# The third sum of weight blocks moves from VectorE to GpSimd in a two-block transformer kernel, and the opening splits its first gate block before it sums

## The chip, the cores and the metric

The kernel runs on one core of a Trainium2 chip. The metric is device time in microseconds (us) of one execution, the median of three runs. TensorE is written PE, VectorE DVE, ScalarE ACT, GpSimd POOL and SyncE SP.

## The reference

Two blocks follow each other, each of two layers, on 256 tokens of width 1024, all in float32. The first block's layer has a feed-forward part (FFN), a mixer of neighbourhood attention and a Fourier transform, and a second FFN; the second block's layer has a mixer of four parts and one FFN. So there are six FFNs:

```python
def swiglu(x, w_in, w_out):
    gu = x @ w_in
    g, u = jnp.split(gu, 2, axis=-1)
    return (jax.nn.silu(g) * u) @ w_out

for l in range(DEPTH):
    x = x + 0.5 * swiglu(rms_norm(x, ffn1_norm[l]), ffn1_w_in[l], ffn1_w_out[l])
    x = x + mixer(rms_norm(x, mix_norm[l]), ...)
    x = x + 0.5 * swiglu(rms_norm(x, ffn2_norm[l]), ffn2_w_in[l], ffn2_w_out[l])
...
    x = x + (jax.nn.silu(gate) * up) @ w_down[l]
```

with `w_in` of 1024 x 5632 and `w_out` of 2816 x 1024.

## The kernel before

**Three products for one.** A float32 weight block `w` is split into `whi` (rounded to the fast matmul type fp32r, by ACT) and `wlo` = `w` - `whi` (by DVE); the activations are split in the same way (`xTh`, `xTl`, `bTh`, `bTl`). Each product is three matmuls: hi by hi, hi by lo and lo by hi (lines L2263 to L2265).

**Units.** The weights of an FFN stream through three slots of 128 x 2048 as 42 "units". For unit u: SP loads it into `raw` (L602) or into a buffer in `work` (L628), ACT rounds it (`hi`, L1100), DVE takes the rest (`lo`, L1616), PE uses it in 12 or 24 matmuls of 128 x 512. The slot of unit u is free when PE has finished unit u - 3. The semaphores `w_hi_ready`, `w_lo_ready` and `unit_done` count units.

**Fewer products by sums of blocks.** Most of `w_in` is multiplied in three groups (i = 0, 1, 2) in the manner of Strassen: of the four blocks of a group (gate and up, upper and lower half of the rows: gate_k0, gate_k1, up_k0, up_k1) seven products are made, five with a sum of blocks or a block alone that is not straight from `raw`:

```python
SUM_UNITS = ((4, 6, 8, 9, 11, 13, 15), (16, 18, 20, 21, 23, 25, 27), (28, 30, 32, 33, 35, 37, 38))
```

For group i these are units m = 0 to 6: m = 0 is gate_k0; m = 1 is the first sum `w_sum` = gate_k0 + up_k0 (L1631); m = 2 is gate_k1; m = 3 is the second sum `t2` = `w_sum` + up_k1 (L1638); m = 4 is the third sum up_k0 + up_k1 (L1641), which is written into `w_sum` again; m = 5 is up_k1; m = 6 is `t2` with gate_k1 added to it by a DMA that POOL issues (`added_block`, L830). All three sums are 128 x 2048 additions on DVE. PE's results are combined by short DVE instructions that read one operand from PSUM (`combine_z` L1656, `combine_u` L1660, `combine_w` L1664, `combine_up0` L1672, `combine_gate1` L1676). `form` and `form_lo_part` (L1710, L1714) make the matching sums of activations, once for each FFN; `product` (L1687) and `pair_product` (L1681) are the gated products.

**Order.** Every engine's program is written out by hand and runs in order. On DVE, within group i, the third sum stands behind `combine_z(i)` and, in group 0, behind two more splits. PE's unit m = 4 of a group starts with a wait for `combine_w(i)`. SP loads up_k0 of the next group when the third sum of this one is done, and up_k1 of the next group when the lo part of m = 5 is done. In the first FFN (f = 0, `start`), the first group's gate and up blocks are loaded after the opening's chunks. POOL's program holds small norm instructions, DMA issues for the attention tables (`spread_table`, seven of them, each waiting for one unit of PE; `attention_bias`, 16 pairs, likewise, in the first FFN of each layer of the first block), four mask additions and `added_block`.

Of the kernel before, what the change touches and what calls it, by code (L numbers as in the profile page):

```python
# [23 lines left out]
ALU = mybir.AluOpType  # L24
# [53 lines left out]
Z_AT, U_AT, W_AT, UP1_AT, UP0_AT, GATE1_AT = 1, 2, 3, 4, 5, 6  # L78
SUMS = 3
T1_AT, T2_AT, T3_AT = 1, 2, 3  # L80
FORMS = 4
# [95 lines left out]
class Signals:  # L177


    def __init__(self, sem):  # L180
# [18 lines left out]
        self.gain_f_landed = sem("gain_f_landed")  # L199
        self.gate_bias_landed = sem("gate_bias_landed")  # L200
        self.small_landed = sem("small_landed")
# [148 lines left out]
def build(nc, a, out):  # L350

    with ExitStack() as ctx:
# [66 lines left out]
        zw, up1 = xn[:, 0, 0:BANK], xn[:, 0, BANK:D]  # L419
        up_k0, up_k1, w_sum, t2 = (area(at, UNIT) for at in (4096, 6144, 8192, 10240))  # L420
        x_full = xn[:, :, :].rearrange("p t d -> p (t d)").rearrange("p (k t n) -> p k t n", k=KC, t=TT)
# [140 lines left out]
        def _(sp):  # L562
# [31 lines left out]
            def ffn(w_in, w_out, l, rnd, f, beside={}):  # L594
# [65 lines left out]
                for i in range(GROUPS):  # L660
                    if i:
                        sp.wait_ge(s.w_sum_ready, SUMS * (GROUPS * f + i - 1) + T3_AT)
                    if rnd == 0 and i == 0:
                        sp.wait_ge(raw_landed[0], 64)
                    up_block(i, 0, up_k0)
                    gate_block(i, 0)
                    if i:
                        sp.wait_ge(s.w_lo_ready, unit(0, rnd) + SUM_UNITS[i - 1][5] + 4)
                        up_block(i, 1, up_k1)
                    plain(2 + i, 0)  # L670
                    if i == 0:
                        up_block(i, 1, up_k1)
                    plain(2 + i, 1)
                    gate_block(i, 1)
                    for d in range(3 * i, 3 * i + 3):
                        if d != 2 + 3 * i or i < GROUPS - 1:
                            down(d)
# [3 lines left out]
            for l in range(DEPTH):  # L681
# [19 lines left out]
                def gate_bias(t, half):  # L701
                    at = half * D
                    broadcast(gate[:, t, at:at + D], "mix_gate_bias", l * 2 * D + at, D, s.gate_bias_landed)

# [86 lines left out]
        def _(pool):  # L791
# [20 lines left out]

            def spread_table(l, rnd):

                with nc.allow_non_contiguous_dma(reason="rows of 64 keys"):
                    for dr in range(NA_DR):
                        pool.wait_ge(s.unit_done, unit(1, rnd) + dr + 4)
                        src = bass.AP(tensor=a["na_rpb"].tensor,
                                      offset=l * (NA_H * RPB_R * RPB_C) + (dr + 8 - GRID_H) * RPB_C + RPB_C // 2,
                                      ap=[[RPB_R * RPB_C, NA_H], [-1, GRID_W], [1, GRID_W]])  # L820
                        dst = spread[:, l * NA_H:(l + 1) * NA_H, dr * GRID_W:(dr + 1) * GRID_W]
                        pool.dma_start(dst.rearrange("q h k -> h q k"), src).then_inc(s.rpb_spread, LOADED)

            def added_block(name, l, rnd, i):
# [8 lines left out]
            def attention_bias(l, rnd):  # L833
# [3 lines left out]
                for j in range(BANDS):  # L837
                    for row in range(GRID_H):
                        if (j, row) == (2, 1):
                            added_block("ffn1_w_in", l, rnd - 4, 1)  # L840
# [8 lines left out]
            for l in range(DEPTH):  # L849
                (r1, _, _, _), (r2, _, _, _) = ffn_stages_a(l)  # L850
                norm(3 * l)
                if l == 0:
                    spread_table(0, r1)
                added_block("ffn1_w_in", l, r1, 0)
                attention_bias(l, r1 + 4)
                pool.wait_ge(s.consts_a_landed, 16)
                pool.wait_ge(s.bias_landed, 2 * BANDS * GRID_H * LOADED * (l + 1))
# [32 lines left out]
                if l + 1 < DEPTH:  # L890
                    spread_table(l + 1, r2)
                for i in range(GROUPS):
                    added_block("ffn2_w_in", l, r2, i)
            pool.wait_ge(s.gain_m_landed, 16 * (DEPTH + 1))
# [7 lines left out]
            for l in range(DEPTH):  # L902
# [102 lines left out]
        def _(act_e):  # L1005
# [85 lines left out]
            def ffn(rnd, f, n, o):  # L1091
# [15 lines left out]
                def summed_hi(i, m):  # L1107
                    source, at = {1: (w_sum, T1_AT), 3: (t2, T2_AT), 4: (w_sum, T3_AT), 6: (t2, 0)}[m]
                    if at:
# [402 lines left out]
        def _(v):  # L1512
# [94 lines left out]
            def ffn(rnd, f, n, o, factor, start=False, next_gain=None):  # L1607
# [13 lines left out]
                def summed_lo(i, m):  # L1621
                    lo(SUM_UNITS[i][m], {1: w_sum, 3: t2, 4: w_sum, 5: up_k1, 6: t2}[m])

# [9 lines left out]
                def second_sum(i):  # L1633
# [4 lines left out]
                    v.tensor_tensor(t2, w_sum, up_k1, ALU.add).then_inc(s.w_sum_ready, 1)  # L1638

                def third_sum(i):  # L1640
                    v.tensor_tensor(w_sum, up_k0, up_k1, ALU.add).then_inc(s.w_sum_ready, 1)  # L1641

# [89 lines left out]
                form_lo_part(1)  # L1732
                first_sum(0)
                for i in range(GROUPS):
                    qa, qb = PLAIN_UNITS[2 + i]
                    loaded_lo(SUM_UNITS[i][0])
                    if i == 0:
                        product_lo(0)
                    loaded_lo(qa)
                    if i == 0:  # L1740
# [16 lines left out]
                    combine_z(i)  # L1757
                    if i == 0:
                        summed_lo(i, 3)
                        loaded_lo(DOWN_UNITS[3 * i])  # L1760
                        third_sum(i)
                        product(2 + i, 0)
                    else:
                        third_sum(i)
                        product(2 + i, 0)
                        summed_lo(i, 3)
                        loaded_lo(DOWN_UNITS[3 * i])
                    if i:
                        product_lo(3 * i)
                    product(2 + i, 1)  # L1770
                    combine_u(i)
                    summed_lo(i, 4)
                    if i:
                        product_lo(3 * i + 1)
                    combine_w(i)
                    loaded_lo(DOWN_UNITS[3 * i + 1])
                    summed_lo(i, 5)
# [57 lines left out]
            def mixer_a(l, next_gain):  # L1835
# [31 lines left out]
                v.wait_ge(s.bias_masked, BANDS * (l + 1))  # L1867
                v.wait_ge(s.gate_bias_landed, 64 * l + 64)

# [1039 lines left out]
```

## Time and profile before

| | |
|---|---|
| median of 3 runs | 1581.43 us (1580.72 to 1581.44) |
| the profiled execution | 1581.31 us, its span 1579.5 us |
| PE busy | 1563.9 us, 99% |
| DVE busy | 1274.1 us, 81% |
| ACT busy | 902.0 us, 57% |
| POOL busy | 219.9 us, 14% |
| mean granted PE clock | 0.999 |
| third sums on DVE | 18, mean 2.28 us |

The span is what the profiler saw; the execution's own time is 1.8 us longer. An engine's rows are stamped with start and duration. The ends of matmuls are modelled: a 128 x 512 matmul is shown as 0.39 us, while the next one starts 0.23 us after it. So a pause of PE is 0.16 us longer, start to start, than the idle time shown. DVE's instructions are shown to start up to 0.1 us before the one ahead of them ends.

### The profile page before, as it was taken

How to read it: one execution, taken by the hardware profiler on the slowest of the kernel's cores; microseconds unless marked ns; L12 is line 12 of the kernel's file. 1: busy time of each engine (PE TensorE's matmuls, PEld its weight loads, DVE VectorE, ACT ScalarE, POOL GpSimd, SP SyncE). 2: the span in 40 equal slices, each digit the busy share in tenths (PEclk: the TensorE clock that was granted, in tenths of full speed). 3: DMA queues.
4: the chain of work that ended last, by engine and by line, in shares of the span. 5: the costliest groups of instructions: out<-in, count | busy, mean ns of one | idle time of the engine just before them, and what ended most of it. 6: DMA issues, size and time to landing. Idle time of an engine off the chain costs nothing.

```text
span 1579.5 us, 18791 instructions
## 1 busy us (share of the span) xinstructions
PE 1563.9 (99%) x7346; PEld 1294.5 (82%) x7346; DVE 1274.1 (81%) x1181; ACT 902.0 (57%) x1000; POOL 219.9 (14%) x271
## 2 busy tenths in 40 slices
PE   8999999999999999999999999999999999999998
PEld 6888888888888888888888888888888888888886
DVE  7888856679887989875677988778898876798886
ACT  7555555646555655555565655566655556665554
POOL 1132112011000113211201000131200002110000
PEclk9999999999999999999999999999999999999999
DMA  9987665558766778766456776561877565277662
GB/s 302 279 230 219 230 210 164 185 183 248 246 196 177 241 233 248 215 223 212 156 178 211 255 237 211 161 220 54 266 231 230 191 192 172 96 260 231 192 210 91
DMA packets 182415, 327.29 MB, mean 207 GB/s; under 512 B 13028, under 2 KB 77944, under 8 KB 182328
## 3 DMA queue, kind: packets, MB, share of 16 engines
q1 hardware_dynamic: 169064, 300.66, 57.2%
q0 software_dynamic: 12960, 24.94, 8.7%
q8 instruction: 58, 0.95, 0.3%
q10 hardware_dynamic: 304, 0.50, 0.1%
q14 instruction: 29, 0.24, 0.0%
HBM read 322.88 MB, written 2.88 MB: 206 GB/s over the span
## 4 chain that ended last, share of the span: by engine, by line
PE 92%; DVE 3%; ACT 2%; issue 1%; DMA 1%; SPq 0%; POOLq 0%; POOL 0%; ACTq 0%; DVEq 0%
PE pg L2263 19%; PE pg L2265 19%; PE pg L2264 19%; PE acc L2263 9%; PE acc L2265 9%; PE acc L2264 9%; PE pg L2384 2%; ACT whi L1100 1%; PE pg L2276 1%; DVE wlo L1616 1%; DVE work L1641 1%; DMA raw<-in_ffn_w_in 1%; PE acc L2557 0%; PE acc L2539 0%; PE acc L2728 0%
## 5 line engine op out<-in xcount | busy, mean ns | idle before, releaser
L2263 PE MATMUL pg<-whi,xTh 128*128 128x512 f32 (+1 forms) x1096 | 436.2, 398 | 4.2 <-DVE wlo L1616 2.5
L2265 PE MATMUL pg<-whi,xTl 128*128 128x512 f32 (+1 forms) x1096 | 426.5, 389 | 0.0
L2264 PE MATMUL pg<-wlo,xTh 128*128 128x512 f32 (+1 forms) x1096 | 425.7, 388 | 0.0
L1616 DVE TENSOR_TENSOR wlo<-raw,whi 128x2048 fp32r<-128x2048 f32 x143 | 328.8, 2299 | 52.4 <-ACT whi L1100 48.7
L1100 ACT ACTIVATE whi<-raw 128x2048 fp32r<-128x2048 f32 x143 | 274.1, 1917 | 153.7 <-PE pg L2265 99.4
L1516 DVE TENSOR_TENSOR wlo<-raw,whi 128x2048 fp32r<-128x2048 f32 (+1 forms) x87 | 198.5, 2282 | 59.4 <-ACT whi L1012 59.2
L2263 PEld LDWEIGHTS pg<-whi,xTh 128*128 128x128 f32 x1096 | 205.9, 188 | 48.9 <-DVE wlo L1616 3.0
L2265 PEld LDWEIGHTS pg<-whi,xTl 128*128 128x128 f32 x1096 | 205.7, 188 | 42.5
L2264 PEld LDWEIGHTS pg<-wlo,xTh 128*128 128x128 f32 x1096 | 206.1, 188 | 40.0 <-issue 1.0
L1616 DVE TENSOR_TENSOR wlo<-work,whi 128x2048 fp32r<-128x2048 f32 x90 | 208.2, 2313 | 31.4 <-ACT whi L1100 31.4
L2263 PE MATMUL acc<-whi,bTh 128*128 128x512 f32 (+1 forms) x572 | 227.2, 397 | 0.0
L1100 ACT ACTIVATE whi<-work 128x2048 fp32r<-128x2048 f32 x90 | 172.5, 1917 | 90.9 <-PE acc L2265 50.9
L2265 PE MATMUL acc<-whi,bTl 128*128 128x512 f32 (+1 forms) x572 | 222.8, 389 | 0.0
L2264 PE MATMUL acc<-wlo,bTh 128*128 128x512 f32 (+1 forms) x572 | 222.3, 389 | 0.0
L1012 ACT ACTIVATE whi<-raw 128x2048 fp32r<-128x2048 f32 (+1 forms) x87 | 165.0, 1899 | 61.8 <-PE acc L2265 37.0
L2265 PEld LDWEIGHTS acc<-whi,bTl 128*128 128x128 f32 x572 | 107.3, 188 | 22.9
L2263 PEld LDWEIGHTS acc<-whi,bTh 128*128 128x128 f32 x572 | 107.5, 188 | 21.4 <-DVE bTl L1694 0.7
L2264 PEld LDWEIGHTS acc<-wlo,bTh 128*128 128x128 f32 x572 | 107.6, 188 | 20.6
L1156 ACT ACTIVATE bTh<-pg 128x512 fp32r<-128x512 f32 x66 | 39.3, 596 | 75.6 <-PE pg L2384 75.6
L2263 PE MATMUL pg<-whi,bTh 128*128 128x512 f32 (+1 forms) x178 | 70.1, 394 | 3.0 <-DVE xn L1664 3.0
L2265 PE MATMUL pg<-whi,bTl 128*128 128x512 f32 (+1 forms) x178 | 69.2, 389 | 0.0
L2264 PE MATMUL pg<-wlo,bTh 128*128 128x512 f32 (+1 forms) x178 | 69.1, 388 | 0.0
(276 smaller groups left out, 1962.0 us busy)
## 6 DMA issues: line engine op xcount, KB each, us to landing
raw<-in_ffn_w_in SPq DMA_DIRECT2D x124, 512.0 KB, 5.6
raw<-in_ffn_w_out SPq DMA_DIRECT2D x88, 512.0 KB, 4.5
raw<-in_mix_w_in SPq DMA_DIRECT2D x64, 512.0 KB, 4.7
raw<-in_w_gate_up SPq DMA_DIRECT2D x64, 512.0 KB, 5.4
work<-in_ffn_w_in SPq DMA_DIRECT2D x48, 512.0 KB, 5.8
raw<-in_w_down SPq DMA_DIRECT2D x44, 512.0 KB, 4.4
work<-in_ffn_w_in POOLq DMA_DIRECT2D x24, 512.0 KB, 8.5
raw<-in_w_in SPq DMA_DIRECT2D x24, 512.0 KB, 5.4
```

Of the source, the lines that this page charges most:

```text
L1012: act_e.activation(whi[:, slot, 0:cols], raw[:, slot, 0:cols], ACT.Copy).then_inc(s.w_hi_ready, 1)
L1100: act_e.activation(whi[:, u % SLOTS, :], source, ACT.Copy).then_inc(s.w_hi_ready, 1)
L1156: act_e.activation(bTh[:, part, :], bank[:, :].rearrange("p (c n) -> p c n", c=2), ACT.Copy).then_inc(s.actT_hi, 1)
L1516: v.tensor_tensor(wlo[:, slot, 0:cols], raw[:, slot, 0:cols], f32(whi[:, slot, 0:cols]), ALU.subtract)\
L1616: v.tensor_tensor(wlo[:, u % SLOTS, :], source, f32(whi[:, u % SLOTS, :]), ALU.subtract).then_inc(s.w_lo_ready, 1)
L1641: v.tensor_tensor(w_sum, up_k0, up_k1, ALU.add).then_inc(s.w_sum_ready, 1)
L2263: pe.matmul(dst, xh, wh, start=first and i == 0, stop=False, skip_group_check=onto)
L2264: pe.matmul(dst, xh, wl, start=False, stop=False, skip_group_check=onto)
L2265: mm = pe.matmul(dst, xl, wh, start=False, stop=last and i == len(pairs) - 1, skip_group_check=onto)
L2276: tr = pe.transpose(pg[b][t][:, c * P:(c + 1) * P], xn[:, t, at:at + P], ident[:, :])
L2384: tr = pe.transpose(bank[:, c * T + t * P:c * T + (t + 1) * P], source[:, t, at + c * P:at + (c + 1) * P], ident[:, :])
```

## The change

The third sum gets a buffer of its own, `t3`, at the free place 2048 of `work`, a semaphore of its own, `third_ready`, and is made by POOL. It is released when both up blocks have landed (and for i > 0 when the previous third sum's lo part is done), rather than by its place in DVE's order. `w_sum` and its counter keep two sums. SP waits for the second sum and the third before it reloads up_k0. In group 0 the two `product`s of the group's plain block move behind `combine_w(0)`. In the first FFN, SP loads the gate block before the up block, DVE makes the lo part of unit 4 before the first sum that also reads that block, and SP waits for the first sum before it overwrites the slot. `gate_bias_landed` is merged into `chunk_landed[3]` to free the semaphore.

```diff
-SUMS = 3
-T1_AT, T2_AT, T3_AT = 1, 2, 3
+SUMS = 2
+T1_AT, T2_AT = 1, 2
...
-        up_k0, up_k1, w_sum, t2 = (area(at, UNIT) for at in (4096, 6144, 8192, 10240))
+        t3, up_k0, up_k1, w_sum, t2 = (area(at, UNIT) for at in (2048, 4096, 6144, 8192, 10240))
...
                     if i:
-                        sp.wait_ge(s.w_sum_ready, SUMS * (GROUPS * f + i - 1) + T3_AT)
+                        sp.wait_ge(s.w_sum_ready, SUMS * (GROUPS * f + i - 1) + T2_AT)
+                        sp.wait_ge(s.third_ready, GROUPS * f + i)
                     if rnd == 0 and i == 0:
                         sp.wait_ge(raw_landed[0], 64)
-                    up_block(i, 0, up_k0)
-                    gate_block(i, 0)
+                        gate_block(i, 0)
+                        up_block(i, 0, up_k0)
+                    else:
+                        up_block(i, 0, up_k0)
+                        gate_block(i, 0)
...
+                    if rnd == 0 and i == 0:
+                        sp.wait_ge(s.w_sum_ready, T1_AT)
                     gate_block(i, 1)
...
                     for dr in range(NA_DR):
+                        if dr == 4:
+                            third_sum(f, rnd, 0)
                         pool.wait_ge(s.unit_done, unit(1, rnd) + dr + 4)
...
+            def third_sum(f, rnd, i):
+
+                for half in range(2):
+                    pool.wait_ge(chunk_landed[half], 16 + 32 * (GROUPS * f + i + 1))
+                if i:
+                    pool.wait_ge(s.w_lo_ready, unit(0, rnd) + SUM_UNITS[i - 1][4] + 4)
+                pool.tensor_tensor(t3, up_k0, up_k1, ALU.add).then_inc(s.third_ready, 1)
...
                     for row in range(GRID_H):
+                        if (j, row) == (1, 2):
+                            third_sum(2 * l, rnd - 4, 1)
                         if (j, row) == (2, 1):
...
                 if l == 0:
-                    spread_table(0, r1)
+                    spread_table(0, r1, 0)
+                else:
+                    third_sum(2 * l, r1, 0)
                 added_block("ffn1_w_in", l, r1, 0)
                 attention_bias(l, r1 + 4)
+                third_sum(2 * l, r1, 2)
...
                 for i in range(GROUPS):
+                    if i or l + 1 == DEPTH:
+                        third_sum(2 * l + 1, r2, i)
                     added_block("ffn2_w_in", l, r2, i)
...
                 for i in range(GROUPS):
+                    third_sum(2 * DEPTH + l, ffn_stage_b(l)[0], i)
                     added_block("w_gate_up_2", l, ffn_stage_b(l)[0], i)
...
-
-                def third_sum(i):
-                    v.tensor_tensor(w_sum, up_k0, up_k1, ALU.add).then_inc(s.w_sum_ready, 1)
...
-                first_sum(0)
+                if start:
+                    loaded_lo(SUM_UNITS[0][0])
+                    first_sum(0)
+                else:
+                    first_sum(0)
+                    loaded_lo(SUM_UNITS[0][0])
...
                     combine_w(i)
+                    if i == 0:
+                        product(2, 0)
+                        product(2, 1)
```

DVE's program at the opening of the first FFN, before. `xn`, `bTh`, `raw`, `work` and `whi` are buffers in SBUF, `pg` is PSUM; L1714 is `form_lo_part`, L1631 the first sum, L1616 a lo split (units 4 and 5 here), L1694 `product_lo`, L1687 `product(1, ...)`, L1638 the second sum:

```order
L1714 TENSOR_TENSOR bTl<-xn,bTh 128x512 x2
L1631 TENSOR_TENSOR work<-raw,work 128x2048
L1616 TENSOR_TENSOR wlo<-raw,whi 128x2048
L1694 TENSOR_TENSOR bTl<-pg,bTh 128x512
L1616 TENSOR_TENSOR wlo<-raw,whi 128x2048
L1687 SCALAR_TENSOR_TENSOR work<-pg,rstd,work 128x256 x2
L1638 TENSOR_TENSOR work<-work 128x2048
```

And of the change (L1737, L1642, L1657, L1717, L1710 and L1664 of the changed kernel are the same instructions):

```order
L1737 TENSOR_TENSOR bTl<-xn,bTh 128x512 x2
L1642 TENSOR_TENSOR wlo<-raw,whi 128x2048
L1657 TENSOR_TENSOR work<-raw,work 128x2048
L1717 TENSOR_TENSOR bTl<-pg,bTh 128x512
L1642 TENSOR_TENSOR wlo<-raw,whi 128x2048
L1710 SCALAR_TENSOR_TENSOR work<-pg,rstd,work 128x256 x2
L1664 TENSOR_TENSOR work<-work 128x2048
```

The split of unit 4 and the first sum have changed places; what follows is as it was.

DVE's program from `combine_z(0)` (L1656) to `combine_w(0)` (L1664) of any FFN, before; L1641 is the third sum, the two L1687 the products of the plain block:

```order
L1656 TENSOR_TENSOR xn<-pg,p 128x512
L1616 TENSOR_TENSOR wlo<-work,whi 128x2048
L1616 TENSOR_TENSOR wlo<-raw,whi 128x2048
L1641 TENSOR_TENSOR work<-work 128x2048
L1687 SCALAR_TENSOR_TENSOR xn<-pg,rstd,xn 128x256 x2
L1660 TENSOR_TENSOR p<-pg,p 128x512
L1616 TENSOR_TENSOR wlo<-work,whi 128x2048
L1664 TENSOR_TENSOR xn<-xn,pg 128x512
L1616 TENSOR_TENSOR wlo<-raw,whi 128x2048
```

And of the change:

```order
L1679 TENSOR_TENSOR xn<-pg,p 128x512
L1642 TENSOR_TENSOR wlo<-work,whi 128x2048
L1642 TENSOR_TENSOR wlo<-raw,whi 128x2048
L1683 TENSOR_TENSOR p<-pg,p 128x512
L1642 TENSOR_TENSOR wlo<-work,whi 128x2048
L1687 TENSOR_TENSOR xn<-xn,pg 128x512
L1710 SCALAR_TENSOR_TENSOR xn<-pg,rstd,xn 128x256 x2
L1642 TENSOR_TENSOR wlo<-raw,whi 128x2048
```

The sum is gone and the two products stand behind `combine_w`.

POOL's program in the first FFN, before; L822 are the issues of `spread_table`, L830 `added_block`, L847 `attention_bias`, L864 the mask additions:

```order
L805 TENSOR_TENSOR rstd<-ms,neghalf 128x1
L822 DMA rpb_spread<-in_na_rpb 8x64x64 x7
L830 DMA work<-in_ffn_w_in 128x2x512 x2
L847 DMA shared<-rpb_spread 16x4x256 x18
L830 DMA work<-in_ffn_w_in 128x2x512 x2
L847 DMA shared<-rpb_spread 16x4x256 x14
L864 TENSOR_TENSOR shared<-shared,consts_a 128x16x32
```

And of the change, where L838 is the third sum:

```order
L811 TENSOR_TENSOR rstd<-ms,neghalf 128x1
L830 DMA rpb_spread<-in_na_rpb 8x64x64 x4
L838 TENSOR_TENSOR work<-work 128x2048
L830 DMA rpb_spread<-in_na_rpb 8x64x64 x3
L846 DMA work<-in_ffn_w_in 128x2x512 x2
L865 DMA shared<-rpb_spread 16x4x256 x12
L838 TENSOR_TENSOR work<-work 128x2048
L865 DMA shared<-rpb_spread 16x4x256 x6
L846 DMA work<-in_ffn_w_in 128x2x512 x2
L865 DMA shared<-rpb_spread 16x4x256 x14
L838 TENSOR_TENSOR work<-work 128x2048
L885 TENSOR_TENSOR shared<-shared,consts_a 128x16x32
```

The three sums stand behind the issue that waits for unit 4, behind the pair that waits for unit 17, and behind the pair that waits for unit 27.

## Rows read from the trace of the kernel before

**Rows 1.** The page: busy time of each engine, share, instructions

```profile
PE 1563.9 (99%) x7346; PEld 1294.5 (82%) x7346; DVE 1274.1 (81%) x1181; ACT 902.0 (57%) x1000; POOL 219.9 (14%) x271
```

**Rows 2.** Waits of PE: us in total, times, longest us

```profile
PE pg L2263 <- DVE xn L1664: 3.0, 6, 0.5
PE pg L2263 <- DVE wlo L1616: 2.5, 1, 2.5
```

**Rows 3.** Timeline, opening: ACT on unit 4, `product(1)`, PE's units 5 and 6

```profile
29.34 1.90 ACT L1100 ACTIVATE whi<-raw 128x2048 fp32r<-128x2048 f32 x1
...
29.89 2.29 DVE L1631 TENSOR_TENSOR work<-raw,work 128x2048 f32<-128x2048 f32 x1
...
37.09 0.87 DVE L1687 SCALAR_TENSOR_TENSOR work<-pg,rstd,work 128x256 f32<-128x256 f32 x2
...
38.02 0.50 PE L2263 MATMUL pg<-whi,xTh 128*128 128x512 f32 x1 [0.57 <-DVE work L1687]
...
44.06 0.39 PE L2263 MATMUL pg<-whi,bTh 128*128 128x512 f32 x1
```

**Rows 4.** Groups of POOL's additions by size: xcount | busy us, mean ns

```profile
L885 POOL TENSOR_TENSOR work<-work 128x126 f32<-128x126 f32 x8 | 3.6, 452 | 0.0
...
L877 POOL TENSOR_TENSOR work<-work 128x512 f32<-128x512 f32 x2 | 2.6, 1296 | 0.2
```

**Rows 5.** Timeline, POOL's first two mask additions beside DVE

```profile
147.60 2.29 DVE L1616 TENSOR_TENSOR wlo<-work,whi 128x2048 fp32r<-128x2048 f32 x1 [0.26 <-ACT whi L1100]
...
148.15 2.88 POOL L864 TENSOR_TENSOR shared<-shared,consts_a 128x512 f32<-128x512 f32 x1 [15.19 <-PE pg L2265]
150.02 3.16 DVE L1616 TENSOR_TENSOR wlo<-raw,whi 128x2048 fp32r<-128x2048 f32 x1
...
154.03 1.29 POOL L864 TENSOR_TENSOR shared<-shared,consts_a 128x512 f32<-128x512 f32 x1 [0.56 <-PE pg L2265]
...
154.10 0.67 DVE L1660 TENSOR_TENSOR p<-pg,p 128x512 f32<-128x512 f32 x1
```

**Rows 6.** Line L628, load of up_k1(0), third FFN: issue times, landing

```profile
L628 SPq DMA_DIRECT2D work<-in_ffn_w_in x2: 469/488/508, 532.3 to 532.9; - x2
...
DMA to landing us min/median/max: 6.0/6.4/6.8
```

**Rows 7.** Timeline, third FFN: lo part of unit 5, and PE on it

```profile
545.29 2.28 DVE L1616 TENSOR_TENSOR wlo<-raw,whi 128x2048 fp32r<-128x2048 f32 x1
...
548.52 0.40 PE L2263 MATMUL pg<-whi,xTh 128*128 128x512 f32 x1
```

**Rows 8.** Timeline, second FFN: fourth issue of `spread_table`, lo of unit 6, PE

```profile
369.35 0.80 POOL L822 DMA_DIRECT2D rpb_spread<-in_na_rpb  x1 [2.48 <-PE pg L2265]
370.32 2.28 DVE L1616 TENSOR_TENSOR wlo<-work,whi 128x2048 fp32r<-128x2048 f32 x1
...
374.31 0.39 PE L2263 MATMUL pg<-whi,bTh 128*128 128x512 f32 x1
```

**Rows 9.** Timeline, first FFN, group 2: POOL behind unit 27, `combine_gate1`, PE's unit 30

```profile
131.95 1.02 POOL L847 DMA_DIRECT2D shared<-rpb_spread  x2 [1.71 <-PE pg L2265]
...
133.19 0.68 DVE L1676 TENSOR_TENSOR p<-pg,p 128x512 f32<-128x512 f32 x1
...
139.65 0.39 PE L2263 MATMUL pg<-whi,bTh 128*128 128x512 f32 x1
```

**Rows 10.** Timeline, first FFN, group 1: POOL behind unit 17, `pair_product`, PE's unit 20

```profile
92.27 1.01 POOL L847 DMA_DIRECT2D shared<-rpb_spread  x2 [4.42 <-PE pg L2265]
...
93.21 0.74 DVE L1681 SCALAR_TENSOR_TENSOR work<-xn,rstd,work 128x512 f32<-128x512 f32 x1
...
99.97 0.39 PE L2263 MATMUL pg<-whi,xTh 128*128 128x512 f32 x1
```

**Rows 11.** Timeline, second FFN, group 1: first sum, and PE's unit 15

```profile
402.03 2.28 DVE L1631 TENSOR_TENSOR work<-raw,work 128x2048 f32<-128x2048 f32 x1
...
411.20 0.39 PE L2263 MATMUL pg<-whi,xTh 128*128 128x512 f32 x1
```

More of the change, by code:

```diff
@@ L199, in __init__ @@
         self.gain_f_landed = sem("gain_f_landed")
-        self.gate_bias_landed = sem("gate_bias_landed")
+        self.third_ready = sem("third_ready")
         self.small_landed = sem("small_landed")
@@ L702, in gate_bias @@
                     at = half * D
-                    broadcast(gate[:, t, at:at + D], "mix_gate_bias", l * 2 * D + at, D, s.gate_bias_landed)
+                    broadcast(gate[:, t, at:at + D], "mix_gate_bias", l * 2 * D + at, D, chunk_landed[3])
                 ffn("ffn1_w_in", "ffn1_w_out", l, r1, 2 * l,
@@ L811, in norm, with spread_table @@
                           2 * n + t + 1)
-            def spread_table(l, rnd):
+            def spread_table(l, rnd, f):
                 with nc.allow_non_contiguous_dma(reason="rows of 64 keys"):
                     for dr in range(NA_DR):
+                        if dr == 4:
+                            third_sum(f, rnd, 0)
                         pool.wait_ge(s.unit_done, unit(1, rnd) + dr + 4)
@@ L890, in _ @@
                 if l + 1 < DEPTH:
-                    spread_table(l + 1, r2)
+                    spread_table(l + 1, r2, 2 * l + 1)
                 for i in range(GROUPS):
+                    if i or l + 1 == DEPTH:
+                        third_sum(2 * l + 1, r2, i)
                     added_block("ffn2_w_in", l, r2, i)
@@ L1107, in summed_hi @@
                 def summed_hi(i, m):
-                    source, at = {1: (w_sum, T1_AT), 3: (t2, T2_AT), 4: (w_sum, T3_AT), 6: (t2, 0)}[m]
-                    if at:
+                    source, at = {1: (w_sum, T1_AT), 3: (t2, T2_AT), 4: (t3, 0), 6: (t2, 0)}[m]
+                    if m == 4:
+                        act_e.wait_ge(s.third_ready, GROUPS * f + i + 1)
+                    elif at:
                         act_e.wait_ge(s.w_sum_ready, SUMS * (GROUPS * f + i) + at)
@@ L1621, in summed_lo @@
                 def summed_lo(i, m):
-                    lo(SUM_UNITS[i][m], {1: w_sum, 3: t2, 4: w_sum, 5: up_k1, 6: t2}[m])
+                    lo(SUM_UNITS[i][m], {1: w_sum, 3: t2, 4: t3, 5: up_k1, 6: t2}[m])
                 def sums_before(i):
@@ L1732, in ffn @@
                 form_lo_part(1)
-                first_sum(0)
+                if start:
[4 more added lines that the diff above has]
+                    loaded_lo(SUM_UNITS[0][0])
                 for i in range(GROUPS):
                     qa, qb = PLAIN_UNITS[2 + i]
-                    loaded_lo(SUM_UNITS[i][0])
                     if i == 0:
                         product_lo(0)
+                    else:
+                        loaded_lo(SUM_UNITS[i][0])
                     loaded_lo(qa)
@@ L1757, in ffn @@
                     combine_z(i)
[L1758 to L1761, printed above, removed]
+                    if i:
                         product(2 + i, 0)
[L1763 to L1767, printed above, removed]
+                    summed_lo(i, 3)
+                    loaded_lo(DOWN_UNITS[3 * i])
                     if i:
                         product_lo(3 * i)
-                    product(2 + i, 1)
+                        product(2 + i, 1)
                     combine_u(i)
@@ L1867, in mixer_a @@
                 v.wait_ge(s.bias_masked, BANDS * (l + 1))
-                v.wait_ge(s.gate_bias_landed, 64 * l + 64)
+                v.wait_ge(chunk_landed[3], LOADED + 64 * l + 64)
                 def add_gate_bias(g, t):
```

## The prediction

> **What bounds the kernel now.** The page first: PE is busy 1563.9 of 1579.5 us and DVE 81% of them [rows 1]. A faster DVE can therefore give back only the pauses of PE, so the waits of PE come next. They are few: six times 0.5 us for `combine_w` (L1664), in group 0 of each FFN, and once 2.5 us for the lo part of unit 4 in the opening [rows 2]; 0.6 us more follows there at unit 5, for `product(1)` [rows 3]. A pause is 0.16 us longer from start to start than the idle time shown, so the six are worth 6 x 0.66 = 4.0 us. The second reading is the slack: how long after its lo part is ready PE first uses a unit. It is small all along. For unit 5 of the third FFN it is 548.52 - 547.57 = 0.95 us [rows 7]. Only 0.06 us of that is needed, the time from a lo part's end to PE's start. Whatever delays DVE by more than about a microsecond there stops PE.
>
> **Removing the third sum from DVE.** 18 instructions of 2.28 us leave DVE, and in group 0 two products move behind `combine_w`. That frees more than 3 us ahead of `combine_w(0)`, and all six waits of 0.66 us go: **-4.0 us**. Nothing else is returned, since PE waits for DVE nowhere else outside the opening.
>
> **The opening.** Unit 4's hi part ends at 29.34 + 1.90 = 31.24. Before, DVE filled the time with the first sum from 29.89 [rows 3]; now the lo part of unit 4 stands first and has to wait until 31.27. PE starts unit 4 at 33.6 rather than 34.43, but it also needs `product(1)` for unit 5, which is at the end of the same row of work (first sum, lo parts of 4 and 5, products): that row starts 31.27 - 29.89 = 1.38 us later, so unit 5 starts at 39.40 rather than 38.02 [rows 3]. The swap of loads on SP moves neither, as ACT took unit 4 without a wait for its landing. The new wait of SP (first sum, done at about 35.8) is ahead of unit 8, which ACT takes much later. Price **+1.4 us**.
>
> **What the sum costs on POOL.** No addition of 128 x 2048 on POOL is in the trace. 126 columns take 0.452 and 512 take 1.296 us [rows 4], 2.19 ns a column, so 2048 take about 4.66 us, twice DVE's 2.28. POOL has the time: a busy share of 14%. The result is wanted by ACT for unit m = 4, more than 10 us after its blocks have landed, so its lateness costs nothing, and nothing behind it on POOL's queue is pressed (the next `spread_table` issue is 6 us away, `added_block` later).
>
> **What it costs DVE.** The mask additions show it [rows 5]. POOL's starts at 148.15 while DVE's split (both operands in SBUF) runs to 149.89, and it takes 2.88 us instead of 1.29: its work is done from 149.89 to 151.03. DVE's next split, at 150.02, takes 3.16 instead of 2.29 us: it is held until about 150.89. So the two exclude each other while both read two operands from SBUF; the one that comes second waits to the end of the first. `combine_u` at 154.10, with one operand in PSUM, takes its 0.67 us in the middle of POOL's next addition: such instructions pass. Held time for 512 columns is 1.00 us (149.89 to 150.89), so for 2048 it is 1.00 + 1536 x 0.00219 = **4.4 us**. Bounds: below, 0, if large additions should not hold DVE; above, 5.2, if the columns cost what the 512 cost with their fixed part, 1.296/512 x 2048. The row that is nearest, 512 columns with its held time, decides for 4.4.
>
> The Trainium skill says the same in "SBUF — State Buffer", section "Who interferes with whom": a DVE instruction with two SBUF inputs contends with a GpSimd instruction that reads SBUF, and the second fully blocks. By that rule, the trace agrees (2.88 and 3.16 us). Its page "GPSIMD Engine Reference", section 3.1, gives 4497 ns for this very addition; the sum would be some 2 us lower by it.
>
> **Where the 18 sums fall**, each by the order of POOL and the landings:
>
> - *Group 0 of FFNs 3 to 6.* The up blocks land by 532.9 + 6.8 = 539.7 [rows 6] and POOL waits for nothing else. DVE works there without a gap, nearly all of it with two SBUF operands. POOL gets in behind the instruction that runs, and all behind it is 4.4 + 0.08 us late. Unit 5's lo part is ready at 547.57 + 4.48 = 552.05 and PE starts at 552.11 instead of 548.52 [rows 7]: 3.6 us, four times, **+14.4**.
> - *Group 0 of FFN 2* starts behind the fourth `spread_table` issue, 369.35 + 0.80 = 370.15, while DVE's second sum runs to 370.40. Unit 6's lo part ends at 370.40 + 4.4 + 2.28 = 377.08, PE starts at 377.14 instead of 374.31 [rows 8]: **+2.8**.
> - *Group 0 of FFN 1*, likewise, on the shifted opening: unit 5's lo part ends at 37.17 + 1.38 = 38.55 and POOL gets in; the products (PSUM) pass, the second sum is held to 42.95, unit 6's lo part ends at 47.4 and PE starts at 47.5 instead of 44.06 [rows 3]: 3.4, of which 1.4 is the opening's, so **+2.0**.
> - *Group 2 of FFNs 1 and 3* starts at 132.97 [rows 9], gets in at 133.27 behind unit 29's split; `combine_gate1` passes. `pair_product`, second sum and unit 30's split follow from 137.67: 0.74 + 2.2 + 2.2 = 142.8, PE at 142.9 instead of 139.65 [rows 9]. 3.2 us, twice, **+6.4**.
> - *Group 1 of FFNs 1 and 3* is requested at 93.28 [rows 10], held off by `pair_product` to 93.95, and keeps unit 20's split (2.29) until 98.35: ready 100.64, PE at 100.70 instead of 99.97 [rows 10]. 0.7 us, and 0.1 more at unit 21: twice, **+1.7**.
> - *Groups 1 and 2 of FFNs 2, 4, 5, 6*: up_k1 lands during the first sum, POOL gets in at 404.31, and unit 15's split is ready at 404.31 + 4.4 + 2.28 = 410.99, just under the 411.14 that PE needs [rows 11]. **0**, and 0.1 each for every 0.1 us over.
>
> **Sum.** -4.0 + 1.4 + 14.4 + 2.8 + 2.0 + 6.4 + 1.7 = +24.7 us. The profiled execution took 1581.31 us for its span of 1579.5, the median is 1581.43; I add to the median: **1606 us**, slower by 1.6%. A measurement of this kernel tells 0.2% (3.2 us) from no change.
>
> **Rivals.**
> - *POOL gets in only when DVE leaves the port on its own* (a gap or a PSUM instruction). For it: no back-to-back pair of large splits around a POOL addition is in the rows. It changes places, not kind: group 0 costs 3.0 us rather than 3.6 four times, and 2.3 rather than 2.8: 1603. It belongs to the likeliest case; together 75%, range 1599 to 1611.
> - *The long addition does not hold DVE*, and the change does what its parts do: -4.0 + 1.4 = -2.6, 1579, within 0.2%. It ends ahead of before by more than 0.2% only if the opening costs under 0.8 us. Against it stand rows 5. It decides from a held time of 1.4 us downward: there the group-0 terms (4 x 0.6) and the opening's 1.4 just cancel the 4.0. 8% for it.
> - *Part of the holds fall elsewhere*, because landings and POOL's waits shift by a microsecond or DVE resumes earlier than at POOL's end: 1586 to 1599. 7%.
> - *PE's clock falls in the pauses.* The granted clock was 0.999 in the mean, and the longest wait was 2.5 us [rows 2]; now seven pauses are 2.8 us and more. If the low level (1.2 for 2.4 GHz) then lasted as long as such a pause, 3.5 us, half of it would be lost: 7 x 1.75 = 12, 1618. Nothing in the rows shows a fall after the 2.5 us. 10%.
>
> **The range.** 1606 as the likeliest; 1592 to 1618 holds its own range, most of the displaced holds and part of the clock's case. Faster 0.03 and same 0.07 are the second rival and half a step of the third; slower 0.90.
>
> **What would show it right.** The waits for L1664 gone; 18 POOL additions of 4.6 us and more; beside each a DVE instruction of 2.28 us shown as up to 6.7; new waits of PE for lo parts of about 3.4 us at units 4 and 5 of FFNs 3 to 6 together, 2.7 at unit 6 of FFN 2, 3 at unit 30 of FFNs 1 and 3; unit 5 of FFN 1 at 39.4. It is wrong if DVE's splits keep 2.3 us beside POOL, if the additions are much shorter, or if PE's clock shows a dip.

## The result and the profile after

The changed kernel takes 1618.28 us (median of 4 runs, 1616.74 to 1621.09) against 1581.43: 1.0236 times as long, with a 95% interval of 1.0223 to 1.0249. The profiled execution's span is 1617.1 us, 37.6 more than before. 1606 was forecast, with 1592 to 1618 around it: the side is right, the size is 12 us short, and the measured time lies just outside the range.

The page of the changed kernel, busy time of each engine as in [rows 1]:

```profile
PE 1578.7 (98%) x7346; PEld 1302.8 (81%) x7346; DVE 1296.5 (80%) x1163; ACT 903.0 (56%) x1000; POOL 305.7 (19%) x289
```

DVE has 18 instructions fewer and is shown busy 22 us longer, and PE, with as many matmuls, 15 us longer. The first is the hold on DVE. The second can't come from waits; it is matmuls that themselves ran slower.

PE's waits in the changed kernel, as in [rows 2] (total us, times, longest us):

```profile
PE pg L2289 <- DVE wlo L1642: 25.5, 11, 3.3
PE pg L2289 <- DVE work L1710: 3.4, 2, 2.8
PE acc L2352 <- DVE bTl L2272: 2.0, 1, 2.0
PE pg L2289 <- DVE bTl L1717: 1.0, 1, 1.0
```

No wait for `combine_w` (now L1687) is left. Eleven waits for lo parts (L1642) stand in place of one. The third row is the start of the kernel.

Timeline of the changed kernel, DVE, POOL and PE (start us, length us, engine, line, operation, [idle before it <- what released it]). In order of time: the opening; first FFN, groups 1 and 2; second FFN, group 0; third FFN, group 0; fourth FFN, group 0 and then group 1:

```profile
30.66 2.29 DVE L1642 TENSOR_TENSOR wlo<-raw,whi 128x2048 fp32r<-128x2048 f32 x1 [1.30 <-ACT whi L1124]
...
33.00 0.50 PE L2289 MATMUL pg<-whi,xTh 128*128 128x512 f32 x1 [1.69 <-DVE wlo L1642]
...
38.79 0.79 PE L2289 MATMUL pg<-whi,xTh 128*128 128x512 f32 x1 [2.78 <-DVE work L1710]
...
95.87 5.26 DVE L1704 SCALAR_TENSOR_TENSOR work<-xn,rstd,work 128x512 f32<-128x512 f32 x1
95.95 4.61 POOL L838 TENSOR_TENSOR work<-work 128x2048 f32<-128x2048 f32 x1
...
136.60 4.77 POOL L838 TENSOR_TENSOR work<-work 128x2048 f32<-128x2048 f32 x1
136.81 0.68 DVE L1699 TENSOR_TENSOR p<-pg,p 128x512 f32<-128x512 f32 x1
137.41 4.53 DVE L1704 SCALAR_TENSOR_TENSOR work<-xn,rstd,work 128x512 f32<-128x512 f32 x1
...
146.49 0.47 PE L2289 MATMUL pg<-whi,bTh 128*128 128x512 f32 x1 [3.05 <-DVE wlo L1642]
...
378.75 6.92 POOL L838 TENSOR_TENSOR work<-work 128x2048 f32<-128x2048 f32 x1
378.90 2.29 DVE L1642 TENSOR_TENSOR wlo<-work,whi 128x2048 fp32r<-128x2048 f32 x1
381.11 0.69 DVE L1717 TENSOR_TENSOR bTl<-pg,bTh 128x512 fp32r<-128x512 f32 x1
381.70 6.12 DVE L1642 TENSOR_TENSOR wlo<-raw,whi 128x2048 fp32r<-128x2048 f32 x1
...
387.88 0.50 PE L2289 MATMUL pg<-whi,xTh 128*128 128x512 f32 x1 [2.12 <-DVE wlo L1642]
...
550.59 4.71 POOL L838 TENSOR_TENSOR work<-work 128x2048 f32<-128x2048 f32 x1 [6.22 <-DMA work<-in_ffn_w_in]
550.73 6.73 DVE L1657 TENSOR_TENSOR work<-raw,work 128x2048 f32<-128x2048 f32 x1
...
559.72 0.50 PE L2289 MATMUL pg<-whi,xTh 128*128 128x512 f32 x1 [3.33 <-DVE wlo L1642]
...
561.19 0.63 PE L2291 MATMUL pg<-whi,xTl 128*128 128x512 f32 x1
561.62 0.63 PE L2289 MATMUL pg<-whi,xTh 128*128 128x512 f32 x1
...
900.25 0.50 PE L2289 MATMUL pg<-whi,xTh 128*128 128x512 f32 x1 [3.33 <-DVE wlo L1642]
...
903.84 0.50 PE L2289 MATMUL pg<-whi,xTh 128*128 128x512 f32 x1 [0.57 <-DVE work L1710]
...
940.07 4.61 POOL L838 TENSOR_TENSOR work<-work 128x2048 f32<-128x2048 f32 x1 [17.18 <-DMA work<-in_ffn_w_in]
940.68 0.69 DVE L1695 TENSOR_TENSOR xn<-pg,xn 128x512 f32<-128x512 f32 x1 [1.08 <-PE pg L2291]
941.29 5.54 DVE L1642 TENSOR_TENSOR wlo<-work,whi 128x2048 fp32r<-128x2048 f32 x1
```

Read the pairs of POOL and DVE first. At 550.59 POOL starts the sum in 4.71 us, and DVE's first sum beside it is shown as 6.73 instead of 2.28 us: 4.45 us of hold. The instruction on PSUM at 136.81 takes its 0.68 us in the middle of POOL's sum, and the next one, with two operands in SBUF, is shown until 141.94, behind the end of POOL's sum at 141.37. Then look at 561.19 and 561.62: two neighbouring matmuls start 0.43 us apart, where 0.23 was usual. That is not a wait.

PE's windows in the changed kernel (stretch, length, PE busy, granted clock, DMA share, GB/s) show it in the clock:

```profile
561.00:563.00 2.00, 2.00 (x6) 0.50 0.87 292
565.00:570.00 5.00, 5.00 (x26) 1.00 0.39 141
900.00:905.00 5.00, 4.18 (x17) 1.00 0.73 238
1176.00:1182.00 6.00, 5.75 (x14) 0.51 0.82 268
1453.00:1459.00 6.00, 6.00 (x16) 0.55 0.85 292
147.90:151.30 3.40, 3.40 (x10) 0.53 0.46 147
670.00:673.60 3.60, 3.60 (x10) 0.53 0.44 105
38.00:42.00 4.00, 3.21 (x8) 0.57 1.04 342
```

Six stretches stand at 0.50 to 0.57, the low level (1.2 GHz), each behind a pause of 2.9 us or more. The stretch at 900 stands at 1.00 behind the same 3.33 us of idle time that comes ahead of 561.

**The 37.6 us, split.** Pauses from start to start, less the usual 0.23 us, add up to 8.8 us before and 32.5 after, 23.7 more. What is left, 13.9 us, goes with the clock: its mean fell from 0.999 to 0.991, so the low level lasted about 0.008 x 1617 / 0.5 = 26 us longer, and half of that is lost, 13 us. Counted matmul by matmul, the stretches with starts 0.43 us apart lose 10.6 us; the starts just behind a pause, also stretched, are not in that count. The four runs point the same way: a mean clock of 0.992 goes with 1616.74 us, 0.991 with 1617.67 and 1618.89, 0.989 with 1621.09.

### The profile page after: what moved, and what is told of

The parts are those of the page before. It is cut to its first block, busy times and chain, and to the rows that moved or that the text cites. A ratio compares the mean times of both kernels' runs of the same rounds, so it can differ in the third digit from the quotient of the medians.

```text
span 1617.1 us, 18823 instructions
## 1 busy us (share of the span) xinstructions
PE 1578.7 (98%) x7346; PEld 1302.8 (81%) x7346; DVE 1296.5 (80%) x1163; ACT 903.0 (56%) x1000; POOL 305.7 (19%) x289
## 4 chain that ended last, share of the span: by engine, by line
PE 84%; DVE 11%; issue 3%; ACT 1%; DMA 0%; POOLq 0%; POOL 0%; DVEq 0%; SPq 0%; ACTq 0%
PE pg L2289 17%; PE pg L2291 16%; PE pg L2290 16%; PE acc L2289 9%; PE acc L2291 9%; PE acc L2290 9%; DVE wlo L1642 3%; DVE work L1657 2%; PE pg L2410 2%; PE pg L2302 1%; DVE work L1664 1%; DVE xn L1725 1%; DVE wlo L1542 1%; DVE xn L1733 1%; DVE work L1704 1%
## 5 line engine op out<-in xcount | busy, mean ns | idle before, releaser
L2289 PE MATMUL pg<-whi,xTh 128*128 128x512 f32 (+1 forms) x1096 | 441.8, 403 | 23.0 <-DVE wlo L1642 19.4
L1642 DVE TENSOR_TENSOR wlo<-raw,whi 128x2048 fp32r<-128x2048 f32 x143 | 332.4, 2325 | 35.7 <-ACT whi L1124 33.0
L1642 DVE TENSOR_TENSOR wlo<-work,whi 128x2048 fp32r<-128x2048 f32 x90 | 227.1, 2524 | 41.6 <-ACT whi L1124 41.6
L838 POOL TENSOR_TENSOR work<-work 128x2048 f32<-128x2048 f32 x18 | 87.9, 4884 | 157.1 <-DMA work<-in_ffn_w_in 79.6
L809 POOL TENSOR_TENSOR ms<-ss,eps 128x1 f32<-128x1 f32 x16 | 19.1, 1197 | 346.4 <-ACT work L1043 346.4
```

Of the source, the lines that this page charges most:

```text
L809: pool.tensor_tensor(sums, mean, eps[:, 0:n], ALU.add).then_inc(ms_sem, 1)
L838: pool.tensor_tensor(t3, up_k0, up_k1, ALU.add).then_inc(s.third_ready, 1)
L1642: v.tensor_tensor(wlo[:, u % SLOTS, :], source, f32(whi[:, u % SLOTS, :]), ALU.subtract).then_inc(s.w_lo_ready, 1)
L2289: pe.matmul(dst, xh, wh, start=first and i == 0, stop=False, skip_group_check=onto)
```

## The experiments

Eight kernels ran, four beside each other on one chip and four on another, each with runs of the kernel before; the changed kernel's time is that of its four runs above. "Theory" is: POOL's addition holds DVE's two-operand SBUF instructions, the lateness makes PE pause, and its clock falls behind some pauses.

**1. POOL writes, but doesn't read.** All queues, waits and counters stay; the third sum is left out, its place is filled with zeros.

```diff
-                pool.tensor_tensor(t3, up_k0, up_k1, ALU.add).then_inc(s.third_ready, 1)
+                pool.memset(t3, 0.0).then_inc(s.third_ready, 1)
```

> The changed kernel, but GpSimd's addition of 128x2048 is replaced by a fill of t3 with zeros, which writes SBUF and reads nothing (the third sum is left out, so unit m = 4 is computed with zeros). Theory (GpSimd's addition reads two SBUF operands and keeps VectorE's two-operand instructions out until it ends; a filling does not): no hold, no pause of TensorE over 1.5 us outside the opening, the six waits for combine_w gone, the opening 1.4 us dearer, granted clock full: 1579 us. Rival 1 (any long GpSimd instruction holds VectorE, whether it reads or not): the fill of 128x2048 took 1.81 us before, so holds of some 1.7 us, and 1583 to 1586 us. Rival 2 (not the hold but the new waits and places in the queues cost the time): near 1618 us.

Measured: 1578.96 us, 0.9984 (0.9975 to 0.9994) of before. In the profiled execution the granted clock is 0.999 and there is no slow stretch. Its timeline in the third FFN:

```profile
539.06 1.81 POOL L838 MEMSET work<- 128x2048 f32 x1 [5.69 <-DMA work<-in_ffn_w_in]
539.73 2.28 DVE L1657 TENSOR_TENSOR work<-raw,work 128x2048 f32<-128x2048 f32 x1
```

POOL's write lies beside the same first sum, which keeps its 2.28 us. So neither the new waits and the place on POOL's queue nor the moved products cost anything beyond the opening's share; all 39 us between this kernel and the changed one hang on POOL's addition. The second rival of the prediction gave 1579 for a change whose sum doesn't hold DVE, and that is what it would have been.

**2. Half the addition.** POOL adds 1024 columns and fills the other 1024 with zeros, so half of the sum is left out.

```diff
-                pool.tensor_tensor(t3, up_k0, up_k1, ALU.add).then_inc(s.third_ready, 1)
+                pool.tensor_tensor(t3[:, 0:UNIT // 2], up_k0[:, 0:UNIT // 2], up_k1[:, 0:UNIT // 2], ALU.add)
+                pool.memset(t3[:, UNIT // 2:UNIT], 0.0).then_inc(s.third_ready, 1)
```

> The changed kernel with an addition of 1024 columns in place of 2048; the other 1024 are filled with zeros (half of the third sum is left out). Theory with two parts (a hold that grows with the columns, 2.15 us here by 1.00 us for 512 and 4.45 us for 2048; and a lower TensorE clock only behind pauses of about 3 us): pauses of 1.3 us four times in group 0 of FFNs 3 to 6, 0.9 us twice in group 2 of FFNs 1 and 3, no dip of the clock outside the opening: 1586 us. Rival (time grows in proportion to the columns, from 1579 at none to 1618 at 2048): 1598 us. Rival (the clock falls behind pauses of 1.3 us too): about 1595 us.

Measured: 1589.96 us, 1.0055 (1.004 to 1.007); in the profiled execution the clock is 0.999 and no pause is followed by a slow stretch. A time in proportion would have been about 1598. The third FFN:

```profile
540.89 2.60 POOL L838 TENSOR_TENSOR work<-work 128x1024 f32<-128x1024 f32 x1 [6.11 <-DMA work<-in_ffn_w_in]
541.14 4.51 DVE L1658 TENSOR_TENSOR work<-raw,work 128x2048 f32<-128x2048 f32 x1
...
547.90 0.50 PE L2290 MATMUL pg<-whi,xTh 128*128 128x512 f32 x1 [1.10 <-DVE wlo L1643]
...
551.49 0.50 PE L2290 MATMUL pg<-whi,xTh 128*128 128x512 f32 x1 [0.53 <-DVE work L1711]
```

The first sum is held 4.51 - 2.28 = 2.23 us, half of 4.45; the pause at unit 4 falls from 3.50 to 1.27 us, by the hold that is gone. The pause at unit 5 doesn't fall: 0.69 to 0.73 us here, 0.73 in the changed kernel at 903.84. The expectation left out these four times 0.7 us, which is most of its miss. They answer to the order of DVE's work (`product(1)` behind unit 5's split), not to how long POOL holds it, once the hold is longer than the slack.

**3. The pauses filled.** Matmuls on operands that are in place, into a bank that the next unit overwrites, stand where PE would be idle; nothing reads them.

```diff
+                def fill(bank, n):
+                    for _ in range(n):
+                        pe.matmul(bank[:, :], xTh[:, 0, 0:P], xTh[:, 0:2, :], start=True, stop=True)
...
+                    if i == 0 and f >= 2:
+                        fill(b_x, 15)
...
+                    if i == 2 and f in (0, 2):
+                        fill(b_y, 13)
```

> The changed kernel, and TensorE runs matmuls that nothing uses where it would pause: 15 of 128x512 (3.4 us) ahead of unit 4 in FFNs 3 to 6, and 13 (3.0 us) ahead of unit 30 in FFNs 1 and 3, into a bank that the next product clears. The result is unchanged. Theory (behind a pause of 3.2 to 3.5 us the granted clock halves for 3 to 5 us, which costs 1.6 to 2.4 us each time beside the pause): the dips at five or six places go and the time falls by 8 to 10 us, to 1608 to 1610 us, with VectorE's holds as they are. Rival (the slower matmuls come from something else, such as weight loads that are late behind the hold): no change, 1618 us, or more.

Measured: 1612.5 us, 1.0199 (1.0184 to 1.0215), 5.8 us less than the changed kernel by the medians and 7.7 by the spans. Its timeline in the third FFN, and two windows:

```profile
554.56 3.56 PE L2407 MATMUL pg<-xTh 128*128 128x512 f32 x15
558.04 0.50 PE L2289 MATMUL pg<-whi,xTh 128*128 128x512 f32 x1
...
561.63 0.50 PE L2289 MATMUL pg<-whi,xTh 128*128 128x512 f32 x1 [0.57 <-DVE work L1710]
```

```profile
558.00:563.00 5.00, 4.43 (x19) 1.00 0.76 242
...
1176.00:1182.00 6.00, 5.78 (x27) 1.00 0.64 241
```

PE does useless work for about as long as it would have waited, unit 4 still starts only when its lo part is there (split ends at 557.99), and the kernel is faster. The clock stays at 1.00 in the stretches that stood at 0.50; one slow stretch is left, in the opening (1.2 us), where nothing was filled. So the low clock is a cost of the idle time, apart from the wait itself. The saving is smaller than the 9.4 us of slow matmuls removed, since the 0.7 us pauses at unit 5, which a slow PE had hidden in three FFNs, now show in all four, and unit 15 of the fourth FFN waits 1.77 instead of 1.04 us.

**4. The same sum at other places.** The sum also waits for PE to finish unit m = 1 of its group, by when DVE has idle time ahead; the whole computation is kept.

```diff
-                        if dr == 4:
+                        if dr == 6:
...
+                pool.wait_ge(s.unit_done, unit(0, rnd) + SUM_UNITS[i][1] + 4)
...
-                        if (j, row) == (1, 2):
+                        if (j, row) == (1, 3):
```

> The changed kernel, but every third sum on GpSimd also waits until TensorE is done with the group's unit m = 1, so that it runs while VectorE has only PSUM instructions or nothing to do (group 0 behind the sixth table issue, group 1 behind the pair for unit 18). The computation is complete. Theory (what costs the time is where the hold falls): the sum gets in behind the lo part of unit m = 2, holds up the lo part of unit m = 3 by 1.0 us or less, pauses of 0.4 us in group 0 and 0.1 us elsewhere, no dips: 1581 to 1583 us. Rival (the hold costs the same wherever it falls, VectorE being short of time): 1605 us or more.

Measured: 1584.18 us, 1.0015 (1.0005 to 1.0025). Its timeline in the third FFN:

```profile
561.77 5.93 POOL L839 TENSOR_TENSOR work<-work 128x2048 f32<-128x2048 f32 x1 [23.59 <-PE pg L2292]
563.14 0.68 DVE L1680 TENSOR_TENSOR xn<-pg,p 128x512 f32<-128x512 f32 x1
566.67 3.19 DVE L1643 TENSOR_TENSOR wlo<-work,whi 128x2048 fp32r<-128x2048 f32 x1 [2.85 <-ACT whi L1125]
```

POOL is asked for while a split runs, gets in behind it at 563.2, and is done at 567.7: the PSUM instruction passes, DVE would have been idle for 2.85 us anyway, and only 0.9 us of hold is left. Of that PE notices 0.40 us, a pause at unit m = 3, ahead of 570.00. Pauses of 0.40 to 0.42 us stand at m = 3 of group 0 in all six FFNs, in place of the six of 0.66 us at m = 4. The additions are as many and on average longer (5.70 us, with their own wait in them), and the kernel is 34 us faster than the changed one. What is left against before, beside these six pauses, stands in the opening (pauses of 1.89 and 2.94 us, and 2.0 us of slow matmuls behind them) and at unit 34 of the first and third FFN (0.92 and 0.93 us).

**5 and 6. The opening by itself.** First the changed kernel with the opening's order undone (loads, SP's wait and DVE's order; the edit to DVE's order is shown), then the kernel before with the new order alone.

```diff
-                if start:
-                    loaded_lo(SUM_UNITS[0][0])
-                    first_sum(0)
-                else:
-                    first_sum(0)
-                    loaded_lo(SUM_UNITS[0][0])
+                first_sum(0)
+                loaded_lo(SUM_UNITS[0][0])
```

> The changed kernel with the opening of the kernel before (up block loaded first, first sum ahead of the lo part of unit 4); third sums on GpSimd. Theory (the opening's new order costs 1.4 us at unit 5, of which the hold of the first sum by GpSimd keeps its own 2 us, and its two pauses of 1.9 and 2.9 us add 1.2 us of lower clock): 1615 to 1616 us, against 1618 of the changed kernel. Rival (the new order of the opening gains, since unit 4 starts 0.8 us earlier): over 1619 us.

Measured: 1617.7 us (1615.25 to 1619.63), 1.0227 (1.0213 to 1.0241). This tells nothing, since the runs overlap with those of the changed kernel. What it does show is in two of its windows:

```profile
387.00:392.00 5.00, 5.00 (x16) 0.66 0.94 265
900.00:905.00 5.00, 4.43 (x10) 0.50 0.67 216
```

Here the clock fell at 900 and behind a 2.27 us pause at 387, where it held in the changed kernel, at pauses of the same length.

> The kernel before with the changed opening alone (gate block loaded and split first; third sums on VectorE). Theory: unit 4 starts 0.8 us earlier and unit 5 1.4 us later, for product(1) stands at the end of the same row of work on VectorE, which now begins 1.4 us later: 1582.8 us, up to 1584 if the clock falls behind the pause of 2.9 us. Rival (an earlier unit 4 is worth its 0.8 us): 1580.6 us.

Measured: 1583.65 us, 1.001 (1.0001 to 1.0019): 1.9 us slower than before, as expected. Unit 5 starts at 39.11 after a pause of 2.94 us, and slow matmuls that cost 1.4 us follow. The eleven runs fall in two groups: five with a mean clock of 0.999 took 1582.2 to 1582.7 us, six with 0.998 took 1583.7 to 1584.8. The profiled one is of the second group. Read so, the same kernel has the clock's loss in some executions and not in others, and the loss is about 1.6 us, near the 1.4 of the slow matmuls.

**7. The sum stays on DVE, but earlier.** In group 0 of the kernel before, the third sum moves straight behind `combine_z(0)`, ahead of the two splits.

```diff
                     if i == 0:
+                        third_sum(i)
                         summed_lo(i, 3)
                         loaded_lo(DOWN_UNITS[3 * i])
-                        third_sum(i)
```

> The kernel before, but group 0's third sum on VectorE stands straight behind combine_z(0), where VectorE waited 2.84 us for the hi part of unit 9; nothing on GpSimd. Theory (the six waits for combine_w(0) come from the place of the third sum, not from VectorE's amount of work): the sum of 2.28 us fits into the wait of 2.84 us, all six waits of 0.66 us go, and nothing is put in their place: 1577.4 us. Rival (VectorE's work in group 0 is too much wherever it stands): 1581 us, with the waits moved to the lo part of unit 9 or 10.

Measured: 1576.82 us (1576.38 to 1577.1), 0.9969 (0.9958 to 0.9981). DVE's timeline in the first FFN:

```profile
48.56 0.68 DVE L1656 TENSOR_TENSOR xn<-pg,p 128x512 f32<-128x512 f32 x1
49.16 2.28 DVE L1641 TENSOR_TENSOR work<-work 128x2048 f32<-128x2048 f32 x1
52.08 2.29 DVE L1616 TENSOR_TENSOR wlo<-work,whi 128x2048 fp32r<-128x2048 f32 x1 [0.64 <-ACT whi L1100]
```

Most of the 2.28 us of the sum fills time in which DVE waited for ACT: 0.64 us of idle time is left behind it. All six waits for `combine_w` are gone, with no work taken from DVE.

PE's unit 4 in the opening of this kernel:

```profile
33.75 0.54 PE L2263 MATMUL pg<-whi,xTh 128*128 128x512 f32 x1 [2.50 <-DVE wlo L1616]
...
34.94 0.63 PE L2263 MATMUL pg<-whi,xTh 128*128 128x512 f32 x1
35.37 0.63 PE L2264 MATMUL pg<-wlo,xTh 128*128 128x512 f32 x1
```

It is the wait of the kernel before, as long as there (2.5 us [rows 2]), but here the starts behind it are 0.43 us apart and the granted clock is 0.50 from 34.1 to 37.4, where the trace of before has 1.00.

**8. With the forms later in the opening.** On top of 7, in the first FFN `form_lo_part(0)` stands behind `product(1)` and `form_lo_part(1)` ahead of parts 2 and 3, so that the first split comes sooner.

```diff
-                form_lo_part(0)
-                form_lo_part(1)
+                if not start:
+                    form_lo_part(0)
+                    form_lo_part(1)
...
+                        if start:
+                            form_lo_part(0)
...
+                        if start:
+                            form_lo_part(1)
```

> e7_early_on_vector, and in the first FFN alone the two form_lo_part instructions (0.65 us each) that stand ahead of the first sum move behind product(1) and behind the lo part of unit 7. Theory (in the opening VectorE is the chain that TensorE waits for): the first sum starts 1.2 us earlier, the lo part of unit 4 is then bound by its hi part (31.24) and comes 0.8 us earlier, and product(1) 0.5 us earlier, so TensorE gains 0.5 us: 1576.9 us. Rival (no gain beyond e7, since the landing of unit 5's block ends the wait): 1577.4 us.

Measured: 1576.05 us (1575.84 to 1576.4), 0.9965 (0.9951 to 0.9978). Unit 4 starts after a pause of 1.96 instead of 2.66 us, and even behind this one the clock stood at 0.50 for a stretch (slow starts from 34.4 on). It is the fastest kernel here, but against 7 the gain of 0.8 us is hardly more than the spread.

## Why the prediction was right in its side and short in its size

**The forecast of the pauses was right.** By its terms, forecast and measured as pauses from start to start:

| term | forecast | measured |
|---|---|---|
| the six waits for `combine_w` | -4.0 | -3.9 |
| opening and group 0 of the first FFN | +3.4 | +2.5 |
| group 0, second FFN | +2.8 | +2.3 |
| group 0, third to sixth FFN | +14.4 | +14.7 |
| group 2, first and third FFN | +6.4 | +6.4 |
| group 1, first and third FFN | +1.7 | +1.7 |
| group 1, second and fourth to sixth FFN | 0 | +1.0 |
| PE's first 21 us, and one small wait at 1429 | none | -1.0 |
| sum (of unrounded terms) | +24.7 | +23.7 |

**The hold.** 4.4 us was forecast from 512 columns and 4.45 measured; the addition takes 4.61 us when nothing holds it, against an estimate of 4.66. The Trainium skill, "SBUF — State Buffer", section "Who interferes with whom", calls the shared ports an exclusive lock and says that issue order decides who blocks. The full block holds here at four times the size (4.45 us beside 2048 columns); for the order, one place differs, where POOL's row starts first and POOL waits ("Who gets in", below). The same section of the Trainium skill says that a GpSimd instruction that only writes doesn't contend with two SBUF inputs of DVE; experiment 1 agrees (2.28 us beside the write). The 4497 ns of the Trainium skill's "GPSIMD Engine Reference", section 3.1, was 0.1 us low: the shortest of the 18 took 4.61.

**Group 0 of FFNs 3 to 6: right sum, wrong step.** The text measured the slack at unit 5's lo part, 0.95 us [rows 7]. But PE needs two things for unit 5, and `product(1)` is the later: the two halves end at 547.49 + 0.87 = 548.36, 0.16 us ahead of PE's start at 548.52, both in the kernel before. The real slack there was almost nothing. So each of these groups loses 3.50 us at unit 4 and 0.73 more at unit 5, 4.2 rather than 3.6; experiments 2 and 3 show the 0.7 four times. In the changed kernel three of the four are hidden by a slow PE, which is why its visible sum comes so near.

**Who gets in.** In the second FFN POOL asks at 378.75, and DVE's next split starts at 378.90, when the second sum ends; it runs its full 2.29 us. POOL comes in at the PSUM instruction at 381.11, and the split behind that is held, by 3.8 us. That is the first rival (POOL gets in only where DVE leaves the port), which gave 2.3 for this place; 2.28 was measured. In group 0 of FFNs 3 to 6 POOL came in between two DVE instructions that both read SBUF twice: in the third it asks at 550.59, 0.13 us ahead of DVE's next row, and that one is held. So the traces show both outcomes at nearly the same lead, and what decides between them is not shown; the start times of the rows alone don't tell who goes first.

**Group 1 of the fourth FFN.** The forecast had 0, "just under the 411.14 that PE needs". In this execution the landing let POOL in at 940.07, 2.76 us behind DVE's first sum instead of 2.28, and the margin of 0.15 us was gone: 1.04 us. A cost at the edge of a landing should have had a value, not a zero.

**The opening.** Unit 5 starts at 38.79 rather than 39.40, since all of the opening came earlier in this execution: ACT's hi part of unit 4 released the split at 30.66, not 31.27. The shift itself, 1.4 us for unit 5, was right; experiment 6 measures 1.9 us for this part with the slow matmuls in it.

**The step that failed is the clock.** It was the fourth rival, with 10%: seven pauses, half of 3.5 us lost behind each, 12 us, 1618. The mechanism was right and its total near: six slow stretches, about 13 us. That 12 and 13 come so close is partly luck, for the places differ (the clock held in the second and fourth FFN and fell in the opening) and each stretch lost 1.2 to 2.4 us, not 1.75. What was wrong is that the sum put the clock at nothing: the likeliest time of 1606 us has no term for it, and 13.9 us were measured. The argument against it was that nothing falls after the 2.5 us wait of before. That is one pause in one execution, shorter than the seven that were forecast, and experiment 7 shows how little it proves: behind the same 2.50 us of idle time the clock stood at 0.50 there. The kernel before holds no pause of 3 us at all, so its trace could not speak against the rival, and the rival should have been added to the likeliest case with, say, half of its weight. As an estimate in hindsight, that gives 1606 + 12 x 0.5 = 1612 and a range that reaches beyond 1618, since each of its terms comes on top of the others and none instead of them.

"TensorE: Matmul & The Clock Gate" in the Trainium skill, section "What's actually happening" of Part 1, tells that the activity that sets the clock is watched in a free-running way, not reset when a kernel starts. The runs agree as far as they go: pauses of equal length (3.33 us of idle time at 559.72 and at 900.25) had a slow stretch behind the one and none behind the other, and in experiment 5 it was different again.

Experiment 3 shows that the idle time brings the clock down, by filling it. Not shown is how the 3 to 4 us between the 10.6 us of counted slow matmuls and the 13.9 us left over are shared between the starts just behind a pause and records that the trace lacks.

## What to carry to other kernels

Moving an instruction from DVE to GpSimd frees DVE only if what runs beside it doesn't need the second SBUF operand: here 2.28 us saved became 4.45 us of hold, and its place on the timeline, not its length, decided whether that cost 37 us or 3. Before giving work to another engine, look for idle time on the engine that has it: experiment 7 took the same six waits away by moving one call up by two lines. When a change is going to make PE pause for 2 to 3.5 us, add the clock's loss to the sum (here 1.2 to 2.4 us behind most pauses of 3 us and more, and behind some of 2 to 3 us). One trace in which the clock held does not show that it will. And when you take a slack from a trace, take the latest of all that the waiting instruction needs.

## What the runs showed of the hardware

- PE's clock fell behind pauses of 1.96 (experiment 8), 2.27 (5), 2.66 (7), 2.94, 3.2 and 3.50 us (the changed kernel) and held behind others of 2.28 and 3.50 (the changed kernel), 2.69 (before) and 2.9 us (1 and 2); two profiled kernels with the same pauses differ in which ones it followed. In the changed kernel a slow stretch of 128 x 512 matmuls has starts 0.427 us apart (0.227 at the full level) and lasts 2.5 to 5.1 us.
- Useless matmuls in a pause made the kernel faster: 5.8 us for six pauses.
- DVE's SCALAR_TENSOR_TENSOR with two tensors in SBUF (L1704, `pair_product`) is held like an addition (5.26 and 4.53 us instead of 0.74); with one operand in PSUM, DVE's instructions took their usual 0.68 us beside POOL.
- When POOL's row starts 0.15 us ahead of DVE's next one, DVE can still go first, and POOL then waits through all of it (6.92 us instead of 4.61); at another place POOL, 0.13 us ahead, went first.
